# Expert lists through eight scatters into a DRAM table, split score products, and another order at the start

## The reference

```python
h = rmsnorm(x, g_mix)
u, q, k, v, gates = split(h @ w_in)          # 512, 512, 128, 128, 2 x 1024 columns
s5 = s5_mixer(u, ...)                        # diagonal complex scan, 32 groups
att = sliding_window_attention(q, k, v, ...) # blocks of 128 queries, 8 heads of 64,
                                             # windows of 2 x 128 keys, ALiBi, sink logit
x = x + merge(s5, att, sigmoid(gates)) @ w_out
t = rmsnorm(x, g_ffn)
coarse = softmax(t @ w_coarse)               # 4 groups, the best one
fine = (t @ w_fine) of that group            # 4 experts in it, the best two
gates = softmax(top_vals) * g_prob
gu = einsum('nd,edf->nef', t, w_up)          # 16 experts, 512 columns each
out = einsum('nef,efd->nd', silu(g) * u * gates, w_down)
x = x + out
```

## Time and profile before

| | before |
|---|---|
| median of 3 runs | 568.95 us (565.61 to 573.72) |
| the profiled execution | 566.51 us, span 564.4 us |
| busy, of the span | TensorE 529.7, VectorE 388.8, ScalarE 280.4, GpSimd 176.4 us |
| mean granted clock of TensorE | 0.974 |
| largest shares of the chain that ended last | TensorE 79%, VectorE 10%, DMA 4%, ScalarE 3% |

### The profile page before, as it was taken

One profiled execution on the slowest core, in us unless ns is written; L12 is line 12 of the kernel. 1 busy time (PEld: TensorE's weight loads), 2 busy tenths in 40 slices (PEclk: granted clock), 3 DMA queues, 4 the chain that ended last, 5 costly groups with the idle time before them and its releaser, 6 DMA issues.

```text
span 564.4 us, 7511 instructions
## 1 busy us (share of the span) xinstructions
PE 529.7 (94%) x2638; PEld 426.1 (75%) x2638; DVE 388.8 (69%) x657; ACT 280.4 (50%) x459; POOL 176.4 (31%) x348
## 2 busy tenths in 40 slices
PE   5999799999999999999999999966999999999992
PEld 3887687887787787777888888955778878777771
DVE  3789384884985975876566733466898887878750
ACT  5544126435445445464233411242677687877841
POOL 1118921089098097000000000003023222434444
PEclk9999899999999999999999999975999999999998
DMA  9640460220220111013357837487999999975532
GB/s 302 116 149 2 101 198 1 75 74 1 76 75 9 66 57 44 14 57 111 111 188 280 316 132 308 176 309 278 366 286 332 337 333 364 357 260 177 138 43 36
DMA packets 62759, 93.95 MB, mean 166 GB/s; under 512 B 14167, under 2 KB 45943, under 8 KB 62722
## 3 DMA queue, kind: packets, MB, share of 16 engines
q1 hardware_dynamic: 56288, 80.84, 41.9%
q0 software_dynamic: 5184, 8.41, 6.8%
q10 hardware_dynamic: 1250, 4.22, 1.9%
HBM read 88.19 MB, written 12.58 MB: 179 GB/s over the span
## 4 chain that ended last, share of the span: by engine, by line
PE 79%; DVE 10%; DMA 4%; ACT 3%; issue 3%; POOL 1%; ACTq 0%; POOLq 0%; DVEq 0%
PE pj L1672 11%; PE pj L1674 10%; PE pj L1673 10%; PE pj L2033 5%; PE pj L2035 5%; PE pj L2034 5%; PE m L2054 5%; PE tp L2019 3%; PE sc L1760 3%; DMA h_rows<-arena_back 1%; PE sc L1759 1%; PE m L2059 1%; PE m L2061 1%; PE m L2060 1%; PE m L1672 1%
## 5 line engine op out<-in xcount | busy, mean ns | idle before, releaser
L1672 PE MATMUL pj<-h_high,split 128*128 128x512 f32 x192 | 76.7, 400 | 0.3 <-DVE h_low L1368 0.3
L1674 PE MATMUL pj<-h_high,split 128*128 128x512 f32 x192 | 74.9, 390 | 0.0
L1673 PE MATMUL pj<-h_low,split 128*128 128x512 f32 x192 | 74.8, 390 | 0.0
L1545 DVE TENSOR_TENSOR up_low<-arena_front,up_high 128x2048 fp32r<-128x2048 f32 x23 | 52.7, 2290 | 11.2 <-ACT up_high L935 11.2
L589 POOL TENSOR_TENSOR rstd<-ssq,half_col 128x1 f32<-128x1 f32 x8 | 4.4, 554 | 161.2 <-DVE ssq L1058 146.2
L2033 PE MATMUL pj<-up_high,xt_high 128*128 128x512 f32 x128 | 51.4, 401 | 0.9 <-DVE xt_low L1579 0.9
L2035 PE MATMUL pj<-up_high,xt_low 128*128 128x512 f32 x128 | 50.8, 397 | 0.0
L2034 PE MATMUL pj<-up_low,xt_high 128*128 128x512 f32 x128 | 50.8, 397 | 0.0
L935 ACT ACTIVATE up_high<-arena_front 128x2048 fp32r<-128x2048 f32 x23 | 44.3, 1929 | 10.6 <-PE pj L2035 9.7
L411 DVE TENSOR_TENSOR split<-arena_front,split 128x2048 fp32r<-128x2048 f32 (+1 forms) x21 | 45.3, 2156 | 0.8 <-ACT split L404 0.6
L689 POOL DMA_INDIRECT out_dram<-arena_back,idx_all x12 | 24.3, 2023 | 62.6 <-DMA out_dram<-arena_back,idx_all 44.9
(11 more groups left out here) (344 smaller groups left out, 1347.7 us busy)
## 6 DMA issues: line engine op xcount, KB each, us to landing
arena_front<-in_w_expert_up_dram SPq DMA_DIRECT2D x23, 1024.0 KB, 11.5
arena_back<-in_w_expert_down_dram SPq DMA_DIRECT2D x16, 1024.0 KB, 10.7
arena_front<-in_w_in_dram SPq DMA_DIRECT2D x13, 1024.0 KB, 5.3
arena_back<-in_w_expert_up_dram SPq DMA_DIRECT2D x9, 1024.0 KB, 12.2
arena_front<-in_w_out_dram SPq DMA_DIRECT2D x4, 1024.0 KB, 5.1
arena_back<-in_x_dram SPq DMA_DIRECT2D x4, 512.0 KB, 5.3
arena_front<-in_w_ssm_glu_gate_dram SPq DMA_DIRECT2D x8, 256.0 KB, 2.6
arena_front<-in_w_ssm_glu_val_dram SPq DMA_DIRECT2D x8, 256.0 KB, 3.3
```

The source lines that it names most:

```text
L1545: tt(up_low[i % NH][:], ring[i % NH], up_high[i % 3][:].bitcast(F32), ALU.subtract).then_inc(up_low_done, 1)
L1672: pe.matmul(dst, sh, mh, start=first and i == 0, stop=False)
L1673: pe.matmul(dst, sh, ml, start=False, stop=False)
L1674: ins = pe.matmul(dst, sl, mh, start=False, stop=last and i == len(terms) - 1)
```

## The change

Three things change at once.

*Lists.* Experts 0 to 3 keep their lists. For experts 4 to 15 VectorE computes in `find_places`, for each token and each of its two experts, the row `place` = place in list x 16 + expert of a table with 128 x 16 rows of two words in DRAM (`list_table`), and the `entries` (token number, gate). GpSimd scatters them in `scatter_places`: eight indirect DMAs of 128 rows of 8 bytes, between gather(2) and gather(3). SP, which has cleared the table with empty entries at the start, reads it back into `lists` and then goes on with its loads. GpSimd waits for that before gather(4). ScalarE waits for `places_done` ahead of `high_down(0)`. `place_lists` and `pick_list` go for these experts.

*Scores.* For a >= 2 (24 of 32 products of q and k) q and k are split (`high_qk` on ScalarE, `low_qk` on VectorE, two operations each) and multiplied in three fp32r products. Their splits take the space of the second `probs` buffer, so the exponentials of a wait until TensorE has turned those of a-1.

*Order.* At the start squares, splits and turned tiles are interleaved in another way on ScalarE, VectorE and TensorE. Both q pieces are split earlier. Before the second norm's rows are stored, SP asks for one half of up weights instead of three. Two semaphores are merged, and one that nobody needs goes.

Line numbers of the changed kernel are larger by 14 to 140.

```diff
 # SP
             load_piece(2)
+            sp.wait_ge(const_ready, 11)
+            sp.dma_start(list_table.rearrange("(p e) w -> p e w", e=NE), lists[:]).then_inc(table_cleared, 16)
             load_piece(3)
...
-            for i in range(5, 8):
-                load_half(i)
+            load_half(5)
             for t in range(TT):
                 sp.wait_ge(h2_stored[t], 16)
+            load_half(6)
             sp.wait_ge(gathered[0], 16)
-            for i in range(8, 10):
+            for i in range(7, 10):
                 load_half(i)
...
+                if e == 0:
+                    sp.wait_ge(scattered, 16 * 2 * TT)
+                    sp.dma_start(lists[:], list_table.rearrange("(p e) w -> p e w", e=NE)).then_inc(lists_loaded, 16)
 # GpSimd
+            def scatter_places():
+                g.wait_ge(table_cleared, 16)
+                g.wait_ge(places_done, 1)
+                for t in range(TT):
+                    for w in range(2):
+                        g.indirect_dma_start(list_table, bass.IndirectOffsetOnAxis(place[:, w, t:t + 1], 0), entries[:, t, w, :], None,
+                                             bounds_check=CAP * NE - 1, oob_is_err=False).then_inc(scattered, 16)
...
-                elif e in LISTS:
-                    g.wait_ge(idx_done, LISTS.index(e) + 1)
+                elif e == 2:
+                    g.wait_ge(idx_done, 2)
+                elif e == LISTED:
+                    g.wait_ge(lists_loaded, 16)
                 gather(e)
+                if e == 2:
+                    scatter_places()
 # ScalarE
             square_rows(0)
+            square_rows(1)
+            square_rows(2)
+            split_high(P_KV)
+            turned_high(0)
+            turned_high(1)
+            square_rows(3)
             act.wait_ge(rows_loaded, 16 * 3)
             act.activation(ldt[:, 1, :], ldt[:, 0, :], ACT.Exp).then_inc(prm_act, 1)
-            square_rows(1)
-            square_rows(2)
+            split_high(P_U)
...
-            turned_high(0)
-            split_high(P_KV)
-            turned_high(1)
-            square_rows(3)
             turned_high(2)
-            split_high(P_U)
             turned_high(3)
...
-                if 1 <= c <= 2:
-                    split_high(P_Q + c - 1)
+                if c == 1:
+                    split_high(P_Q)
+                    split_high(P_Q + 1)
...
+                    if KVH <= a + 1 < NQ:
+                        high_qk(a + 1)
 # VectorE, experts
+            def find_places():
+                rc = lambda w: bc(row_min[:, w, :].rearrange("p (t o) -> p t o", o=1), [P, TT, NE])
+                v.wait_ge(const_ready, 9)
+                link(stt(row_of, pos[:].rearrange("p e t -> p t e"), float(NE), bc(row_no[:].rearrange("p (o e) -> p o e", o=1), [P, TT, NE]),
+                         ALU.mult, ALU.add))
+                link(v.tensor_reduce(row_min[:, 0, :], row_of, AX_X, ALU.min))
+                link(tt(is_row[0], row_of, rc(0), ALU.is_equal))
+                link(stt(other, is_row[0], 65536.0, row_of, ALU.mult, ALU.add))
+                link(v.tensor_reduce(row_min[:, 1, :], other, AX_X, ALU.min))
+                mark(v.tensor_copy(place[:], row_min))
...
+                v.sem_inc(places_done, 1)
...
             for e in range(NE):
-                if 1 <= e <= LAST_LISTS:
-                    read_lists(e + 1)
-                if e < LAST_LISTS:
-                    for n in range(LISTS[e + 2], LISTS[e + 3]):
-                        pick_list(n)
+                if e == 0:
+                    find_places()
+                if e == LISTED:
+                    v.wait_ge(lists_loaded, 16)
...
 # TensorE
             pe.wait_ge(const_ready, 3)
-            for t in range(TT - 1):
+            for t in range(2):
                 turn_tile(t)
-            keys_values(0)
-            turn_tile(TT - 1)
-            for j in range(1, TT):
+            for t in range(2, TT):
+                keys_values(t - 2)
+                turn_tile(t)
+            for j in range(TT - 2, TT):
                 keys_values(j)
...
-                    ins = pe.matmul(dst, qT[ps, hh // 2, t0:t0 + P], kT[ps, kv, t0 + P - W:t0 + P], start=False, stop=True)
+                    if a < KVH:
+                        ins = pe.matmul(dst, qT[ps, hh // 2, t0:t0 + P], kT[ps, kv, t0 + P - W:t0 + P], start=False, stop=True)
+                        continue
+                    pe.matmul(dst, q_high[ps, h // 2, :], k_high[ps, :], start=False, stop=False)
+                    pe.matmul(dst, q_high[ps, h // 2, :], k_low[ps, :], start=False, stop=False)
+                    ins = pe.matmul(dst, q_low[ps, h // 2, :], k_high[ps, :], start=False, stop=True)
...
                 up(e, range(DC))
-                if e < LAST_LISTS:
-                    pe.wait_ge(idx_done, e + 2)
-                    place_lists(LISTS[e + 2], LISTS[e + 3])
```

119 lines of the change are left out of this document (82 added, 37 removed).

## The result

The changed kernel takes 571.62 us in the median of 20 runs (568.09 to 574.07), the kernel before 569.16 (565.61 to 573.72): ratio 1.0038 with a 95% interval of 1.002 to 1.0057. It is slower by 0.4%, where 558.5 was forecast. Medians are of all runs of a kernel; the ratios leave out the few slow ones, which lie more than 1.5% above its fastest. The profiled execution took 572.65 us with a span of 570.9, against 566.51 and 564.4. Of the 6.1 us between the two executions, 2.5 is what the medians show; the rest is that the profiled run of before is 2.65 under its median and this one 1.0 over it.

What follows compares the result with a forecast made beforehand. TensorE, busy 529.7 of 564.4 us, was taken as the bound, with a chain of adds deciding the experts. Start -5.5, scores -2.0, experts -1.7 sum to -9.2: 559.7 as a median, put at 558.5; range 550 to 567.

Steps and rivals of the forecast that it cites:

- Part 1, start: Start to first gate product: K/V product earlier, wait before q products and clock drop behind it gone; -5.5 us (-3.5 to -7.5).
- Part 2, scores: Scores in 24 heads: three fp32r products replace plain fp32, -0.08 us each; -2.0 in all (-6.2 to +2.4).
- rival 3: Start and scores give nothing back: late gate piece, new clock drop, no fp32r gain; -2 for both, about 564; chance 0.08.
- Part 3, loads: Before the first gather: one half load in front instead of three, gather near 377.9; -3.2 us (-2 to -4).
- Part 4, lists: Experts: list products off TensorE, -4.3, but the add chain starts 2.7 later; experts with loads -1.7 (-7.5 to +2.7).
- some of the 0.86 per link can be had: Chain of adds in the experts: eleven links each 0.4 us shorter, 4.4 in all.
- rival 2: Scatters slow: lists at 415 to 419, gathers late, TensorE waits 3 to 5 once; experts +3.5, median 564.5; chance 0.18.
- Rival 4: Slower than before: scatters and table read until 425 or more, experts +10, median 570; chance 0.07.
- the three terms' bad ends: Least favourable bounds of start, scores and experts: -3.5, +2.4 and +2.7 us.
- a risk for four of eight: Scatters on GpSimd: if four of eight meet VectorE's low splits, 5 us more than the 10.4 for all.
- the page's other rule: VectorE in fast mode keeps GpSimd from writing descriptors; every scatter meeting a low split waits, 18 us instead of 10.4 to 15.
- The rule on small transfers: Scatters move 8 bytes each, under the 512 wanted; read-change-write would lengthen landings; no size given.

Runs made afterwards that it cites:

- gate_piece_first: Kernel before with the change's start order and half loads, plus the first gate piece loaded ahead of the sixteen transposing loads; 559.88 us (0.9838).
- scores_alone: Kernel before with only the change's split products of scores and single probs buffer; 571.80 us (1.0040).
- loads_alone: Kernel before with only the change's order of SP's half loads; 565.05 us (0.9920).
- gather_between: Changed kernel with the fourth gather (expert 3) issued between the second and third scatter instead of behind the eighth; 570.87 us (1.0037).
- halves_from_four: Changed kernel with the adds of experts 4 to 15 by halves of a row, instead of those of 12 to 15 alone; 570.50 us (0.9997).
- lists_alone: Kernel before with only the change's lists by scatters; 574.20 us (1.0096).

## Why the prediction was wrong

The forecast was -9.2: start -5.5, scores -2.0, experts -1.7. Measured alone they are -1.1, +2.9 and +1.1 (lists +5.3, loads -4.2), +2.9 in sum where the whole gave +2.5.

*Part 1, start, -5.5.* Measured -1.1. What it said to go did go: K/V products at 15.74, no wait and no low clock at the q products, the gate piece late, a wait of 1.9 in all at the first scores. The step that failed is "Nothing excludes a new clock drop, which costs up to the same 1.8": a drop was treated as an open risk of fixed size. It came behind the very wait that the text foretold and lasted ten microseconds instead of four; behind that wait stand transposes and plain fp32 scores, and not full products as behind the old one. gate_piece_first shows that it was the wait: with it shortened the clock holds and 4.3 us come back, of wait and clock together.

*Part 2, scores, -2.0.* Measured +2.9. The price of a head was right (0.86 for 0.94), and its sum too: 1.6 by the last block. The step that failed is "The four splits ... stand beside a gate product, where both have room", and with it the missing question of who is late next: TensorE meets VectorE's chain at 248.5, where nothing of the gain is left, and more clock is lost in the experts in runs with the splits. What the splits have to do with that clock stays open, and it is the larger part of the miss. The 0.2 for a change of mode stood in no row; the runs bear it out (232.87 to 233.07 in scores_alone, from the last split product to the next head's plain one).

Parts 1 and 2 together are rival 3, which had 0.08: the first gate piece late, a new wait with a drop of the clock, nothing from the short products. It priced them at -2 where they measured +1.8.

*Part 3, loads, -3.2.* Measured -4.2. Right in mechanism. The first gather went at 379.8 in loads_alone, where 377.9 was said, but that run was 1.5 late before the stage began; counted from there it is 0.4 off. The stage got 3.0 shorter in the profiled runs, and the median 4.2, with an interval that holds 3.2.

*Part 4, lists, -4.3 on TensorE and a chain of adds that gives it back.* For the lists the forecast held +1.5 (-1.7 for both parts, of which -3.2 are loads). Measured +5.3 alone, +5.1 within the whole. The mechanism is in the main the one written down: the first add late, one add after the other to the end. The start of the chain was sized well. The first add was said to come at 416.5, 2.7 later than before; it came at 419.15, and with the 3.55 by which the whole stage was late taken off this is 415.6, 1.8 later. The step that failed is "some of the 0.86 per link can be had; I take half, 0.4 x 11 = 4.4": the links are not 0.4 shorter than before but 0.4 longer (10.68 against 10.31), whole adds go 10.3 to 10.8 apart however fast TensorE is, and that term is not 4.4 but nothing or less. In the two profiled runs, counted within the stage, the last whole add comes 5.9 later than before (1.8 and eleven links of 0.37) and the end 3.0 later, where 1.7 sooner was said. "It kept pace with 9.73 in the late steps" was a misreading: in the trace of before, too, the adds from 458.01 to 520.08 are 10.3 us apart beside TensorE's 9.73. They fell from 0.9 to 6.5 behind their outputs, and ScalarE waited only 0.9 for landings in all; the changed kernel's adds begin 6.9 behind. Before, the chain of adds had slack and did not set the end. A second step was left out of the sum: TensorE was to gain 4.3, but it gets the rows of the fourth expert late (a step of 13.2 for 10.6), which stood in rival 2 alone ("TensorE waits 3 to 5 once"; 3.32 measured), with lists that were there by 416.5.

Rival 4 had the right sign, slower than before, but not by its own road: it wanted the table at 421.5 and the first add at 421 to 422 or later, for a loss of 10 in the experts. Nothing of the kind came; the lists and loads cost 1.1 together, and the sign follows since parts 1 and 2 gave +1.8 instead of -7.5. The range ended at 567 because the three terms' bad ends were never added: -3.5, +2.4 and +2.7, each within its own bounds, give 570.5 as a median.

That scatters wait out VectorE's low splits was in the text as a risk for four of eight; five did. The Trainium skill ("SBUF — State Buffer", SBUF: two separate sides) has a VectorE instruction with two inputs in SBUF contend with a GpSimd instruction that reads SBUF, and whichever issues first has the ports. The three pairs of rows above agree, if a scatter's reading of its places counts as such an instruction, which no run here shows. The prediction named the page's other rule, of the fast modes and the writing of descriptors; the same page excepts TENSOR_TENSOR from it and infers that such an operation does not hold up a DMA's descriptors, and there the rows decide against the page. The rule on small transfers ("DMA: Bandwidth & Descriptors", Specifications) shows no clear sign: the last scatter landed in 4.01 us, less than a gather's 4.47 of far larger rows.

## What to carry to other kernels

Before work is taken off the busiest engine, find every chain that runs beside it at nearly the same pace, here adds at 10.3 us beside steps of 9.7 to 10.6, and price the change on that chain first: where it starts, how long a link is, and how far it may fall behind before it holds anyone. Where two or three chains are nearly equally late, an experiment that lifts one alone shows no gain, and that does not clear it. Count times of one trace from the start of the stage before comparing them with another's. A wait that is shortened elsewhere is worth what the next late thing leaves of it, and where that is a new wait of TensorE, the low clock behind it can cost more than the wait. Add up the bad ends of the terms too, since they can all come.

## What was not expected of the hardware

Four more scatters of 128 x 8 bytes cost 8.5 us of the whole kernel, 2.1 each, where one takes 0.98, and 0.30 to the next, when VectorE leaves it alone. Down matrices of 1 MB landed in 10.7 us in the middle before, and in 18.4 in the changed kernel, 24.1 in gather_between and 19.3 in halves_from_four, which move the same weights; single ones took up to 33.0. A wait of 1.9 us in two pieces was followed by ten microseconds of half clock (0.52), and waits of 0.28 and 0.18 at the same place by none (1.00), nor those of 0.50 and 0.18 before. Kernels with the same code up to the router were granted a different clock there: the profiled run of before lost it once up to 374 us (60 to 64), those of lists_alone and loads_alone four times, and the lost clock of single runs of before goes from 14.7 to 23.3 us. A difference of 2 us between two profiled runs of this kernel says nothing without that number beside it.
